# A hybrid attention and expert step: the slot table made on the chip, and modulation chunks on column halves

## What is computed

```python
def trunk_layer(x, mod, n1, n2, ...):                  # once per layer and group
    sh1, sc1, g1, sh2, sc2, g2 = [mod[:, i] for i in range(6)]
    h = rms_norm(x, n1) * (1.0 + sc1) + sh1
    q, k, v, u = split(h @ w_in)                       # attention heads | convolution module
    x = x + g1 * (concat([attention(q, k, v), conv_module(u)]) @ w_out)
    h2 = rms_norm(x, n2) * (1.0 + sc2) + sh2
    return x + g2 * grouped_moe(h2, ...)               # best of 4 groups, 2 experts in it, of 16

def modulation(cvec, w_mod_l, b_mod_l):                # (1024) @ (1024, 6144) + bias
    return (silu(cvec) @ w_mod_l + b_mod_l).reshape(-1, 6, 1024)
```

## Time and profile before

| | us |
|---|---|
| median of 3 runs (1241.38 to 1250.29) | 1241.76 |
| the profiled execution, its own time | 1243.84 |
| its span, from the first instruction to the last | 1242.0 |
| PE busy in the span | 1040.2 |
| DVE busy | 417.2 |
| ACT busy | 158.4 |
| POOL busy | 125.0 |

### The profile page before, as it was taken

One profiled execution on the slowest core, in us unless ns is written; L12 is line 12 of the kernel. 1 busy time (PEld: TensorE's weight loads), 2 busy tenths in 40 slices (PEclk: granted clock), 3 DMA queues, 4 the chain that ended last, 5 costly groups with the idle time before them and its releaser, 6 DMA issues.

```text
span 1242.0 us, 11220 instructions
## 1 busy us (share of the span) xinstructions
PE 1040.2 (84%) x4060; PEld 435.5 (35%) x4060; DVE 417.2 (34%) x1035; ACT 158.4 (13%) x354; POOL 125.0 (10%) x167
## 2 busy tenths in 40 slices
PE   5999999998787988877757999999579788868881
PEld 1244535552132333333314453555223233323330
DVE  0128879444011111101023888944311011101113
ACT  0110234220000000000011023422000000000001
POOL 0010300501110000000022020050210000000001
PEclk9899989998898999989887999998789899989996
DMA  9953971365789796999987334035565999799924
GB/s 334 385 184 134 220 277 68 111 227 124 287 339 402 296 408 243 380 426 424 411 327 271 105 111 162 35 118 205 107 251 225 405 424 387 318 402 424 383 85 169
DMA packets 76181, 328.93 MB, mean 265 GB/s; under 512 B 6550, under 2 KB 9286, under 8 KB 59694
## 3 DMA queue, kind: packets, MB, share of 16 engines
q1 hardware_dynamic: 56528, 277.89, 58.1%
q0 software_dynamic: 8528, 27.51, 6.7%
q10 hardware_dynamic: 11028, 22.23, 5.9%
HBM read 305.48 MB, written 22.13 MB: 264 GB/s over the span
## 4 chain that ended last, share of the span: by engine, by line
PE 55%; DMA 22%; DVE 13%; issue 5%; POOL 3%; ACT 2%; SPq 1%; ACTq 0%; DVEq 0%; POOLq 0%
PE ps L1535 16%; DMA ring<-in_w_up_dram 14%; PE ps L1244 10%; PE ps L1551 8%; PE ps L1261 7%; DVE scr L929 7%; PE ps L1445 7%; DMA ring<-in_w_down_dram 4%; DMA ring<-in_w_mod_dram 1%; PE ps L1370 1%; PE ps L1520 1%; DMA scr<-expert_rows,pick_y 1%; POOL slot_tokens L545 1%; PE ps L1280 1%; DMA slot_rows_sb<-slot_tokens 1%
## 5 line engine op out<-in xcount | busy, mean ns | idle before, releaser
L1535 PE MATMUL ps<-ring,hT 128*64 128x512 f32 x1024 | 250.1, 645 | 56.0 <-DMA ring<-in_w_up_dram 49.0
L1261 PE MATMUL ps<-ring,cs 128*2 128x512 f32 x384 | 185.9, 636 | 12.7 <-DMA ring<-in_w_mod_dram 12.7
L929 DVE SCALAR_TENSOR_TENSOR scr<-scr,convw 128x128 f32<-128x128 f32 (+1 forms) x480 | 160.7, 417 | 0.0
L1535 PEld LDWEIGHTS ps<-ring,hT 128*64 128x64 f32 x1024 | 85.7, 147 | 195.3 <-issue 181.7
L1551 PE MATMUL ps<-ring,scr 128*64 128x512 f32 x624 | 142.8, 598 | 5.8 <-DVE scr L1209 3.0
L1244 PE MATMUL ps<-ring,hT 128*128 128x512 f32 (+1 forms) x384 | 146.1, 541 | 0.0
L1218 DVE TENSOR_TENSOR scr<-ps,scr 128x256 f32<-128x256 f32 x32 | 13.6, 425 | 349.3 <-ACT scr L821 349.3
L1244 PEld LDWEIGHTS ps<-ring,hT 128*128 128x128 f32 x384 | 72.9, 191 | 69.8 <-issue 67.4
L1445 PE MATMUL ps<-ring,hT 128*128 128x512 f32 x192 | 84.4, 594 | 1.3 <-ACT hT L688 1.3
L1261 PEld LDWEIGHTS ps<-ring,cs 128*2 128x2 f32 x384 | 31.2, 88 | 147.9 <-issue 143.3
L1551 PEld LDWEIGHTS ps<-ring,scr 128*64 128x64 f32 x624 | 49.7, 138 | 86.9 <-issue 83.4
(11 more groups left out here) (193 smaller groups left out, 734.7 us busy)
## 6 DMA issues: line engine op xcount, KB each, us to landing
ring<-in_w_gate_dram SPq DMA_DIRECT2D x32, 2048.0 KB, 12.1
ring<-in_w_up_dram SPq DMA_DIRECT2D x32, 2048.0 KB, 16.4
ring<-in_w_down_dram SPq DMA_DIRECT2D x32, 2048.0 KB, 21.4
ring<-in_w_mod_dram SPq DMA_DIRECT2D x22, 2048.0 KB, 14.5
ring<-in_w_in_dram SPq DMA_DIRECT2D x6, 2048.0 KB, 19.7
expert_rows<-scr ACTq DMA_DIRECT2D x78, 128.0 KB, 7.6
ring<-in_w_out_dram SPq DMA_DIRECT2D x4, 2048.0 KB, 14.8
expert_rows<-x ACTq DMA_DIRECT2D x1, 6656.0 KB, 36.1
```

Of the source, the lines that this page charges most:

```text
L929: v.scalar_tensor_tensor(out, span, w, out, ALU.mult, ALU.add).then_inc(conv_step[part_], 1)
L1261: mm = pe.matmul(ps[0:2, mod_bank(l, c), :], cs[:, :, k], slot_w(slot_of(n))[:, k - k0 if split(l, c) else k, :], start=(k == 0), stop=(k ...
L1535: mm = pe.matmul(ps[b * TT:(b + 1) * TT, bank, :].rearrange("p (m n) -> p m n", m=2), tokens(k), w[:, :, k, b * HF:(b + 1) * HF], start=(k ...
```

## The change

The slot table is no longer scattered to DRAM and read back. VectorE turns each of a token's two slot numbers into a row number (its place in a block of 64, plus 64 for the odd expert of a pair) and a column number (pair of experts and block), with shifts and masks on integers. It compares each with a counting matrix (`iota`) into two one-hot marks, the second multiplied by the token number. TensorE adds up the six products of marks in PSUM: this is the table, 128 rows by 48 columns, copied once into `slot_tok`. Gathers for pairs and for overflow both use its columns; an overflow gather fetches 128 rows, of which the transposes take the half of their expert.

A modulation chunk is split into column halves ("lanes"): the vectors are replicated to 64 columns, and two matmuls of 256 columns write PSUM partitions 0 to 63 and 64 to 127. Bias rows, additions and stores follow that layout: rows are 128 partitions by 256 columns per chunk, loaded and stored in two DMAs. Chunks 8 and 9 stay as they were. The first broadcasts use all 128 rows of the array.

The order changes: chunk 10 and half of chunk 11 stand ahead of the positions, the other half and chunk 0 of layer 1 between positions and marks, chunks 1 and 2 behind the marks, chunk 3 behind the transposes of the first gathered rows. VectorE copies the table before the rows and gates are worked out.

```diff
@@ POOL
-            pool.dma_start(slot_rows, slot_rows_sb[:, :]).then_inc(zero_st, 16)
-            pool.wait_ge(zero_st, 16)
...
-                pool.wait_ge(pos_ready, l + 1)
-                for n in range(TILES * 2):
-                    pool.indirect_dma_start(out=slot_dram,
-                                            out_offset=bass.IndirectOffsetOnAxis(ap=pick[:, n:n + 1], axis=0),
-                                            in_=tok_id[:, n // 2:n // 2 + 1], in_offset=None).then_inc(scatter_st, 16)
-                pool.wait_ge(scatter_st, (l + 1) * (2 * TILES * 16))
-                pool.dma_start(slot_rows_sb[:, :], slot_rows).then_inc(slots_in, 16)
                 pool.wait_ge(slots_ready, l + 1)
...
-                        pool.indirect_dma_start(out=ov_x[0:TT, :], out_offset=None, in_=h2_dram,
+                        at = e // 2 * NT + t
+                        pool.indirect_dma_start(out=ov_x, out_offset=None, in_=h2_dram,
...
@@ rows on 128 partitions; lane_out stores them alike, row b * LP + g
+        def lane_in(eng, rows, vec, done):
+            for b in range(LANES):
+                eng.dma_start(rows[b * LP:(b + 1) * LP, :].rearrange("p (c n) -> p c n", n=LW),
+                              vec.rearrange("o (c b n) -> o b c n", b=LANES, n=LW)[:, b].broadcast_to(
+                                  [LP, vec.shape[1] // SEG, LW])).then_inc(done, 16)
@@ DVE
+                step.link(v.tensor_scalar(code_base, slot_base, float(SEG) / CAP, None, ALU.mult))
                 dve.wait_ge(pos_ps, l + 1)
...
+                step.mark(v.tensor_scalar(code[:, 1, :], code[:, 0, :], 3, TT, ALU.logical_shift_right, ALU.bitwise_and))
+                step.link(v.tensor_scalar(code[:, 2, :], code[:, 0, :], TT - 1, None, ALU.bitwise_and))
+                step.link(v.tensor_tensor(row_n, code[:, 1, :], code[:, 2, :], ALU.add))
+                step.mark(v.tensor_scalar(code[:, 1, :], code[:, 0, :], 10, None, ALU.logical_shift_right))
+                step.link(v.tensor_scalar(code[:, 2, :], code[:, 0, :], 6, 7, ALU.logical_shift_right, ALU.bitwise_and))
+                step.link(v.scalar_tensor_tensor(col_n, code[:, 1, :], float(NT), code[:, 2, :], ALU.mult, ALU.add))
+                for n in range(TILES * 2):
+                    t = n // 2
+                    v.tensor_scalar(row_mark[:, n, :], iota[:, :], row_n[:, n:n + 1], None, ALU.is_equal)
+                    v.tensor_scalar(col_mark[:, n, :], iota[:, 0:E // 2 * NT], col_n[:, n:n + 1], tok_id[:, t:t + 1],
+                                    ALU.is_equal, ALU.mult).then_inc(marks_ready, 1)
                 v.tensor_copy(count[0:1, 0:E], ps[0:1, 5, NE:NE + E]).then_inc(pos_ready, 1)
                 mod_take(l, MOD2)
+                mod_take(l, MOD2 + 1)
+                dve.wait_ge(slots_ps, l + 1)
+                v.tensor_copy(slot_tok[:, :], ps[:, 6, 0:E // 2 * NT]).then_inc(slots_ready, 1)
+                if l + 1 < LAYERS:
+                    mod_take(l + 1, 0)
...
@@ TensorE, modulation
+                    for b in range(LANES):
+                        mm = pe.matmul(ps[b * LP:(b + 1) * LP, mod_bank(l, c), 0:LW], cs_rep[:, k, :],
+                                       w[:, b * LW:(b + 1) * LW], start=(k == 0), stop=(k == KD - 1))
@@ TensorE, first broadcasts
-                pe.matmul(ps[:, banks[n], :], ident[0:2, n // 2:n // 2 + 1].broadcast_to([2, P]),
-                          rowA[:, c_ * SEG:(c_ + 1) * SEG], start=True, stop=True).then_inc(first_bc_ps, 1)
+                for b in range(LANES):
+                    mm = pe.matmul(ps[:, banks[n], b * LW:(b + 1) * LW],
+                                   ident[:, b * LP + n // 2:b * LP + n // 2 + 1].broadcast_to([P, P]),
+                                   rowA[:, c_ * LW:(c_ + 1) * LW], start=True, stop=True)
@@ TensorE, routing
-                modulation(l, MOD2, 0, KD // 2)
+                modulation(l, MOD2)
+                modulation(l, MOD2 + 1, 0, KD // 2)
                 pe.wait_ge(sel_ready, l + 1)
...
-                modulation(l, MOD2, KD // 2, KD)
+                modulation(l, MOD2 + 1, KD // 2, KD)
                 if l + 1 < LAYERS:
-                    modulation(l, MOD2 + 1)
                     modulation(l + 1, 0)
-                else:
-                    modulation(l, MOD2 + 1, 0, KD // 2)
-                pe.wait_ge(slots_in, (l + 1) * 16)
...
+                for n in range(TILES * 2):
+                    pe.wait_ge(marks_ready, l * TILES * 2 + n + 1)
+                    mm = pe.matmul(ps[:, 6, 0:E // 2 * NT], row_mark[:, n, :], col_mark[:, n, :],
+                                   start=(n == 0), stop=(n == TILES * 2 - 1))
+                mm.then_inc(slots_ps, 1)
                 if l + 1 < LAYERS:
-                    for c_ in range(1, MOD1):
+                    for c_ in range(1, MOD1 - 1):
...
                 pe.wait_ge(gathered[0], (l * (E // 4) + 1) * 16)
                 xT(0)
+                if l + 1 < LAYERS:
+                    pe.wait_ge(mod_taken, (l + 1) * MODC + 1)
+                    modulation(l + 1, MOD1 - 1)
+                pe.wait_ge(mod_taken, (l + 1) * MODC + (MOD1 if l + 1 < LAYERS else 0))
```

More of the change, by code:

```diff
@@ L37 @@
 MODC = 6 * D // SEG
+LANES = 2
+LW = SEG // LANES
+LP = P // LANES
 SLOTS = 6
@@ L128, in mod_item, with lanes @@
     return MOD_B[l] + c - MODN if c < MOD2 else MOD_G[l] + c - MOD2
+def lanes(c):
+    return c not in (8, 9)
 def mod_bank(l, c):
@@ L844, in mod_take @@
                 if c == 0:
-                    dve.wait_ge(rowA_in, (l + 1) * 32)
+                    dve.wait_ge(rowA_in, (l + 1) * 64)
                 if c == MOD1:
-                    dve.wait_ge(rowC_in, (l + 1) * 16)
+                    dve.wait_ge(rowC_in, (l + 1) * 32)
                 if c == MODN:
-                    dve.wait_ge(rowB_in, (l + 1) * 32)
+                    dve.wait_ge(rowB_in, (l + 1) * 48)
                 if c == MOD2:
-                    dve.wait_ge(rowG_in, (l + 1) * 16)
-                half = slice(c % 2 * SEG, (c % 2 + 1) * SEG)
+                    dve.wait_ge(rowG_in, (l + 1) * 32)
+                w = LW if lanes(c) else SEG
+                half = slice(c % 2 * w, (c % 2 + 1) * w)
                 if c < MOD1:
-                    row = rowA[:, c * SEG:(c + 1) * SEG]
+                    row = rowA[:, c * LW:(c + 1) * LW]
                 else:
@@ L857, in mod_take @@
                 dve.wait_ge(slot_used[slot_of(n)], uses(n))
[L858 removed]
+                v.tensor_tensor(row, ps[:, mod_bank(l, c), 0:LW] if lanes(c) else ps[0:2, mod_bank(l, c), :], row, ALU.add).then_inc(mod_taken, 1)
                 if c // 2 in (1, 4):
@@ L1081, in _ @@
                 runs = [cutr(E // 2 + E) for _ in range(2)]
-                extra, row_base = cutr(E), cutr(E)
+                extra, row_base, code_base = cutr(E), cutr(E), cutr(E)
+                row_n, col_n = cutr(TILES * 2), cutr(TILES * 2)
                 assert o <= D
@@ L1260, in modulation @@
                 for k in range(k0, k1):
-                    mm = pe.matmul(ps[0:2, mod_bank(l, c), :], cs[:, :, k],
-                                   slot_w(slot_of(n))[:, k - k0 if split(l, c) else k, :],
-                                   start=(k == 0), stop=(k == KD - 1))
+                    w = slot_w(slot_of(n))[:, k - k0 if split(l, c) else k, :]
+                    if not lanes(c):
+                        mm = pe.matmul(ps[0:2, mod_bank(l, c), :], cs_rep[:, k, 0:2], w, start=(k == 0), stop=(k == KD - 1))
+                        continue
+                    for b in range(LANES):
+                        mm = pe.matmul(ps[b * LP:(b + 1) * LP, mod_bank(l, c), 0:LW], cs_rep[:, k, :],
+                                       w[:, b * LW:(b + 1) * LW], start=(k == 0), stop=(k == KD - 1))
                 if k1 == KD or split(l, c):
@@ L1343, in _ @@
                                               ident[0:TAPS + 1, 0:TAPS + 1])
+                        if l == 0:
+                            mm = pe.matmul(ps[:, 3, P:2 * P], ones, tri, start=True, stop=True)
                         mm.then_inc(convw_ps, 1)
```

109 lines of the change are left out of this document (52 added, 57 removed).

## The result

The changed kernel takes 1206.3 us (median of 4 runs, 1203.47 to 1210.3), 0.9686 of the kernel before beside it (95% interval 0.9656 to 0.9715). A second set gave 0.9723 (0.9693 to 0.9753). Its profiled execution took 1206.56 against 1243.84: 37.3 less, where the forecast's sum was 46.5. The mean granted clock of TensorE went down, from 0.921 to 0.900.

The account below looks back on a forecast made before the run. Seen as mattering: both layers' routing, where TensorE waits for the scattered table, and the start. Gains 29 + 12 + 7 + 1 - 2.5 = 46.5 off 1243.84 give 1197.3; with the runs' median 2.1 lower, 1195 predicted, range 1181 to 1216.

Parts of the forecast that it names:

- The chunk: Modulation chunk on TensorE: 32 passes in column-half pairs running side by side, 3.6 us instead of 7.03 (bounds 3.4 and 3.9).
- pair rivals: Chunks: loads exposed in pairs, chunk 7.8, about 1234 (6%); or pairs one after another, chunk 11.3, about 1290 (2%).
- The start: Before the first projection: later fifth chunk, but broadcasts over 128 rows at full clock; gain 7 us (bounds 0 and 10).
- Layer 0's routing: Positions to first expert, layer 0: without scatter and read-back, first expert at 315.5 instead of 344.58; gain 29 (bounds 23, 35).
- The 2.2 allowed for a cold chunk: Layer 0, before the first expert: 2.2 us added for a cold clock after TensorE's wait for the gather.
- Layer 1's routing: Positions to first expert, layer 1: rows ready at 899.8 instead of 914.67, first expert's weights at half clock; gain 12 (bounds 6, 18).
- The rotary stretch: Attention: four additions ahead of the taps save 0.25 us each on VectorE, 1.0; cheaper chunks beside the taps buy next to nothing.
- Between the layers: From layer 0 to layer 1: two chunks become cheaper, but TensorE waits for the combine there; gain 0.
- Overflow gathers and experts: Expert stretches: overflow gathers double to 512 KB, 4.9 us of transfer, half falling where weights are awaited; -2.5 us.
- The rival of the weights: Layer 0's routing and experts: weights, gathers and gate row need 40 us of transfer in some 28; price 10 us, 1205 (15%).

## Why the prediction was right, and where its sum was off

**The chunk** (3.6): right, 3.67 and 3.56. The pair rivals fall. By the Trainium skill (TensorE: Matmul & The Clock Gate, Part 3, "The mechanism") a weight load overlaps running matmuls only where the row groups differ; the two halves use the same rows, so their loads should not have been hidden. The rows show otherwise: passes 0.111 apart with a load of 64 columns ahead of each. With exposed loads a chunk would have been 5.1, an estimate from that page's load time. The section also names a background weight buffer as a second case, which the forecast left out and no run here can tell apart.

**The start** (7): right in this pair of profiles, 6.6, and by its own steps: chunk five at 45.85 (45.4), 5.36 for it (5.3), broadcasts 7.17 (6.9). The size is less certain than that looks: three profiles with the old start have 71.8, 71.8 and 74.2, seven with the new one, unaltered, 67.6 to 69.4. Over all of these the gain is 4, so that 7 was met so closely is partly luck. The forecast's 48 KB for the rows before are 33 KB by their shapes (2 partitions of 4096 values), which changes nothing.

**Layer 0's routing** (29, got 26.0): positions at 282.66 are 290.9 on the forecast's clock with the start's and attention's shift of 6.1 and the 2.2 of the position matmuls (291.0); the table is copied at 292 (298.1 on that clock, forecast 298.2). Three terms behind it were too small: the gather took 11.06 (chain of waits, from 292.17) and not 9.5, with the transfers full; the transposes went at half clock, 1.94 for 1.1; and the addition and its wait took 1.50 for 0.6. Together 3.3, where 3.0 are missing. The 2.2 allowed for a cold chunk were right (5.75 for 3.6).

**Layer 1's routing** (12, got 14.1 from the out-projection, 13.2 from the router's end): right, though the 1.5 chunks cost 3.0 more than the old half, not 1.7, at half clock (8.32), and the first expert 9.10, which the forecast had.

**The rotary stretch** (+1.0, got -5.3 in both attentions): the step that failed. Its reading that cheaper chunks buy next to nothing there held: VectorE sets the first maximum, which came 0.3 us sooner in layer 0, and in layer 1 0.9 later in one profile and 0.3 sooner in the other. What the forecast put at nothing, without a reason, is TensorE's clock behind the wait for that maximum. From there to the first head's output layer 1 took 11.1 and 11.6 where it had taken 7.3, and 7.3 again with the wait filled. Undivided chunks did not bring it back (10.5), nor did the moved taps (11.6). That the stretch has two prices stood in the profile before: its layer 0 took 10.4. Which of them layer 1 would pay no row there told, and why the kernel before pays the lower one stays open.

**Between the layers** (0, got -0.9 and 1.4 more within attention 1): TensorE's wait grew from 15.10 to 21.63, and the projections behind it took 22.93 for 21.51. That the longer wait is the cause is not shown: after waits of 15.1 to 15.7 three profiles have 21.51, 21.59 and 22.20, after 18.5 to 21.6 nine have 21.27 to 22.93. With the wait filled it is 20.77. So 0 was right within that spread, and the price of the wait was in the kernel before too.

**Overflow gathers and experts** (-2.5, got -3.3): of the right size, but the stage varies by more than that among the profiles, so nothing is shown by it. The rival of the weights was at work only weakly (waits for in_w_up 21.4 instead of 17.7); it came true when the start of the experts moved another 19 us.

## What to carry to other kernels

Two limits of nearly the same length hide each other: in one stage the table alone gave 13 us, the halves 7, both 26. When work is made cheaper, ask what stood beside it: here taps on VectorE that end no sooner, so that the shorter chunk gained nothing. And ask at which clock the work behind each wait will run, as one stretch cost 7.3 us or 11. Where an engine with a clock of its own waits a few microseconds on the critical path, useless work in the wait can be worth more than the next saving (20 us here, 6 to 7 of them from four matmuls in each layer).

## What was new about the hardware

- Extra work on TensorE shortened the stretch that holds it: 1.5 and 0.65 us of constant matmuls in the router took 4 us off 64.
- Passes of 256 columns with 64-column loads: 0.111 us apart when neighbours alternate between the halves of PSUM's partitions, 0.17 to 0.18 when they don't; the constant matmuls, with the same shape and the same weights, 0.22 (20.02 for 92).
- TensorE, busy without a gap but with two rows of the array, fell to half clock (0.50 from 57.0 on); the same broadcasts over 128 rows kept it.
- In the first head the same instructions behind the same wait of 1.2 us keep full clock in layer 1 of the kernel before, twice (7.3 us), and lose it in its layer 0 and in layer 1 of two variants (10.2 to 11.5). No run explains it.
